# Prompt attention: probabilities transposed by a product with a diagonal of reciprocal row sums

## What is computed

```python
def sparse_attend(q, kg, vg, valid):
    ...
    s = jnp.einsum('btkgd,btjkd->btkgj', qg, kg).astype(jnp.float32) * HEAD_DIM ** -0.5
    s = jnp.where(valid[:, :, None, None, :], s, -1e30)
    pr = jax.nn.softmax(s, axis=-1)
    o = jnp.einsum('btkgj,btjkd->btkgd', pr.astype(vg.dtype), vg)
```

## Time and profile before

| what | value |
| --- | --- |
| time of the kernel, median of 3 runs | 3674.19 us |
| lowest and highest of them | 3671.43 and 3676.53 us |
| span of the profiled execution | 3673.0 us |
| mean granted TensorE clock in it | 0.889 |
| TensorE's matmuls busy | 3060.5 us (83%) |
| VectorE busy | 1360.5 us (37%) |
| ScalarE busy | 741.1 us (20%) |
| GpSimd busy | 933.8 us (25%) |

### The profile page before, as it was taken

How to read it: one execution, slowest core, us unless ns; L and a number is a source line. 1 busy time by engine, 2 the same in 40 slices (tenths; PEclk the granted TensorE clock), 3 DMA queues, 4 the chain that set the end, 5 groups by cost and what they waited for, 6 DMA issues and landing times.

```text
span 3673.0 us, 44605 instructions
## 1 busy us (share of the span) xinstructions
PE 3060.5 (83%) x17464; PEld 2770.9 (75%) x17464; DVE 1360.5 (37%) x1847; ACT 741.1 (20%) x1136; POOL 933.8 (25%) x588
## 2 busy tenths in 40 slices
PE   6999276667799999999999860278888999999996
PEld 5998156666689999999999320134578899999996
DVE  6631644443542222222511177775203422222225
ACT  3321411112110000000200256424311200000001
POOL 2432022220233333333433010000002233333331
PEclk8999678887799999999999575589868999999998
DMA  4111000001211111111211110000122111111111
GB/s 132 46 46 29 17 1 0 0 0 49 76 35 46 46 43 46 46 46 46 90 46 33 50 38 20 0 22 2 55 72 76 32 46 43 46 46 43 46 46 61
DMA packets 237187, 152.44 MB, mean 42 GB/s; under 512 B 21243, under 2 KB 232884, under 8 KB 236169
## 3 DMA queue, kind: packets, MB, share of 16 engines
q1 hardware_dynamic: 226000, 121.17, 11.5%
q10 hardware_dynamic: 11116, 30.33, 2.3%
HBM read 133.46 MB, written 18.01 MB: 41 GB/s over the span
## 4 chain that ended last, share of the span: by engine, by line
PE 69%; DVE 11%; ACT 5%; issue 2%; DMA 0%; DVEq 0%; ACTq 0%; POOL 0%; POOLq 0%
PE ps L1298 50%; ACT junk L815 2%; PE ps L1389 2%; PE ps L1396 2%; PE ps L644 2%; PE ps L713 2%; PE ps L677 1%; PE ps L1347 1%; DVE sc L944 1%; PE ps L1401 1%; DVE hl L2028 1%; ACT dn_yy L1658 1%; PE ps L615 1%; PE ps L746 1%; PE ps L601 1%
## 5 line engine op out<-in xcount | busy, mean ns | idle before, releaser
L1189 POOL TENSOR_TENSOR w_hi<-w_raw,ones 128x512 fp32r<-128x512 f32 (+1 forms) x250 | 370.9, 1484 | 2216.3 <-PE ps L1298 1973.2
L1298 PE MATMUL ps<-xh,w_hi 128*128 128x352 f32 x2928 | 638.4, 326 | 59.3 <-DVE xl L1979 20.7
L1298 PE MATMUL ps<-xh,w_lo 128*128 128x352 f32 x2928 | 634.5, 324 | 0.0
L1298 PE MATMUL ps<-xl,w_hi 128*128 128x352 f32 x2928 | 633.8, 325 | 0.0
L1298 PEld LDWEIGHTS ps<-xh,w_hi 128*128 128x128 f32 x2928 | 502.6, 190 | 63.7 <-issue 59.9
L1298 PEld LDWEIGHTS ps<-xh,w_lo 128*128 128x128 f32 x2928 | 505.8, 189 | 0.0
L1298 PEld LDWEIGHTS ps<-xl,w_hi 128*128 128x128 f32 x2928 | 500.5, 189 | 0.0
L1192 POOL TENSOR_TENSOR w_lo<-w_raw,w_hi 128x512 fp32r<-128x512 f32 (+1 forms) x250 | 480.5, 1922 | 19.6
L2044 DVE TENSOR_TENSOR x<-x,ps 128x1056 f32<-128x1056 f32 x128 | 160.5, 1254 | 501.8 <-PE ps L1298 501.8
L1298 PE MATMUL ps<-hh,w_hi 128*128 128x352 f32 x1536 | 333.0, 325 | 13.7 <-DVE hl L2028 13.7
L1298 PE MATMUL ps<-hh,w_lo 128*128 128x352 f32 x1536 | 331.1, 323 | 0.0
(11 more groups left out here) (363 smaller groups left out, 3100.9 us busy)
## 6 DMA issues: line engine op xcount, KB each, us to landing
w_raw<-in_w_up SPq DMA_DIRECT2D x64, 512.0 KB, 4.1
w_raw<-in_w_down SPq DMA_DIRECT2D x128, 256.0 KB, 2.8
w_raw<-in_w_in_rec SPq DMA_DIRECT2D x24, 512.0 KB, 3.9
x_spill<-x ACTq DMA_DIRECT2D x2, 4224.0 KB, 13.2
x<-x_spill ACTq DMA_DIRECT2D x4, 2112.0 KB, 8.3
w_raw<-in_w_in_att SPq DMA_DIRECT2D x16, 512.0 KB, 3.8
kpg<-in_cache_k SPq DMA_DIRECT2D x64, 128.0 KB, 2.0
vpg<-in_cache_v SPq DMA_DIRECT2D x64, 128.0 KB, 2.0
```

The source lines that it names most:

```text
L1189: pool.tensor_tensor(w_hi[:, j % 2, 0:n], w_raw[:, j % 2, 0:n], ones[:, 0:1].to_broadcast([P, n]), ALU.mult).then_inc(w_hi_done, 1)
L1298: mm = pe.matmul(ps[:, 3 * (j % 2) + t, 0:n], w[:, j % 2, k * P:(k + 1) * P], r[:, k, c0:c0 + n], start=(k == 0 and p == 0), stop=(k == kt ...
```

## The change

The multiplication of pr by the reciprocals is gone. Instead VectorE makes, for each head, a 128x128 diagonal matrix of the reciprocal row sums (scale_q, the identity times the column of reciprocals), with one reciprocal instruction for the four heads. TensorE's transpose of a block of pr becomes an ordinary product of that block with the diagonal matrix, whose result is the transposed block, each query's column scaled by its reciprocal. scale_q has two buffers, for even and odd groups; a new wait keeps VectorE from overwriting one before the value products of the group two before are done. at_nrm now counts diagonals. The samples' attention is unchanged.

```diff
+        scale_q = at("scale_q", [P, 2, GRP, P], F32, M0 + 16 * ROW)
...
                         for g in range(GRP):
-                            mm = pe.transpose(quad(4 + c % 2)[:, g, :], pr[n % 2][:, g, k * P:(k + 1) * P], ident[:, :])
+                            mm = pe.matmul(quad(4 + c % 2)[:, g, :], pr[n % 2][:, g, k * P:(k + 1) * P], scale_q[:, n % 2, g, :],
+                                           start=True, stop=True)
                         mm.then_inc(S["at_tr"], 1)
...
             def normalise(n):
-                w = P * (n // KV + 1)
+                a = n * GRP
+                dve.wait_ge(S["at_exp"], a + GRP)
+                if n >= 2:
+                    dve.wait_ge(S["at_pv"], steps_before[n - 1])
+                own.then(dve.reciprocal(rden[:, a % 8:a % 8 + GRP], den[:, a % 8:a % 8 + GRP]))
                 for g in range(GRP):
-                    a = n * GRP + g
-                    dve.wait_ge(S["at_exp"], a + 1)
-                    own.then(dve.reciprocal(rden[:, a % 8:a % 8 + 1], den[:, a % 8:a % 8 + 1]))
-                    dve.tensor_scalar(pr[n % 2][:, g, 0:w], pr[n % 2][:, g, 0:w], rden[:, a % 8:a % 8 + 1], None, ALU.mult)\
+                    dve.tensor_scalar(scale_q[:, n % 2, g, :], ident[:, :], rden[:, (a + g) % 8:(a + g) % 8 + 1], None, ALU.mult)\
                         .then_inc(S["at_nrm"], 1)
```

## The result

| | median | lowest to highest |
| --- | --- | --- |
| before, 7 runs | 3675.27 us | 3671.43 to 3681.28 |
| after, 7 runs | 3686.35 us | 3683.14 to 3692.16 |
| ratio | 1.0027 | interval 1.0017 to 1.0038 |

The change costs 11.1 us by the medians; 9.3 were predicted. (The ratio and its interval are an estimate of their own, not the quotient of the medians.) The time lies in the range of 3677 to 3692, and 0.4 us above the 3681 to 3686 that were held to be likeliest. The profiled execution of after has a span of 3687.4 us (its own time is 3689.27) and a mean clock of 0.891. Its span is 14.4 longer than that of before, more than the medians are apart, and not all of it comes from the change: the stage's first score product already stands 6.15 later (2364.68 for 2358.53), where both programs are the same. The stage has therefore to be measured from its own start.

What follows compares the result with a forecast made beforehand. In prompt attention VectorE bounds passes 0 to 6, TensorE later ones. VectorE -7.3, early first sets +3.6 and +0.8, open late sets +17.6, clock -5.4 give +9.3 us on 3674.2: 3684, range 3677 to 3692.

Steps and rivals of the forecast that it cites:

- The bounds: Prompt attention: VectorE's queue sets main-loop passes 0 to 6, while masks are built; from pass 7 the chain follows TensorE.
- VectorE's saving: Passes 0 to 6: normalising a group takes 0.99 us at any width, saving 7.3 us; later savings are worth nothing.
- The price of a set: TensorE, four heads' products replacing four transposes: 0.90 us for 0.44, so 0.45 more at full clock, 0.91 at half.
- a product that costs hardly more: Rival, late loop: a product costs hardly more than a transpose, kernel gets faster, 3662 to 3667; chance 0.08, shared with slack.
- that of four times: Rival: a product costs four times a transpose, 1.76 us for four heads; +67 us, 3741; chance 0.02.
- The count of open sets: Passes 7 to 15: 39 four-head groups of products not covered by VectorE's work, at 0.45 us each, 17.6 us.
- The first two sets: Passes 7 to 14: two four-head groups of products need 1.80 us, narrowly covered by VectorE's last maximum and copy, 1.98.
- The new waits: VectorE's waits for earlier value products and for the last of four exponentials before the single reciprocal: cost nothing.
- The first sets: Passes 0 to 6, first four-head products before VectorE's copy: 3.6 us in passes 0, 1, 2, 4; 0.8 in 3, 5, 6.
- The clock: Early passes: shorter TensorE waits remove three of five clock falls of some 1.8 us each, -5.4; bounds none and all.
- The clock does as before: Rival: all five clock falls behind TensorE's early waits stay; +14.7 us, 3689; chance 0.20.
- The clock stays up: Rival: no clock falls from pass 3 on, -10 instead of -5.4; +4.7 us, 3679; chance 0.15.

Runs made afterwards that it cites:

- e1: The changed kernel with the old transposes: VectorE builds diagonals nobody uses, the division by row sums is left out; 3667.12 us, 0.9976 of before.
- e2: The kernel before, VectorE still normalising, with each transpose made by an fp32 product with the identity; 3698.77 us, 1.0063 of before.
- e3: The change for groups 0 to 7 only, groups 8 to 15 as in the kernel before; 3668.96 us, 0.9978 of before.
- e4: The change for groups 8 to 15 only, groups 0 to 7 as in the kernel before; 3693.31 us, 1.0047 of before.
- e5: The kernel before plus unread filling products on TensorE ahead of its waits in groups 3 to 8; 3669.07 us, 0.9981 of before.
- e7: The kernel before with the multiplication by reciprocals of groups 0 to 7 moved to ScalarE, transposes kept; 3655.59 us, 0.9939 of before.

## Why the prediction was right

**The bounds** were read rightly. e1 and e2 show it from both sides: VectorE's saving is worth nothing late (e1: +0.37, all of it the copy's wait in pass 8), and TensorE's price is paid in full there (e2: +17.72). e3 and e4 then put the gain and the loss where the prediction had them.

**VectorE's saving.** A normalisation takes 0.99 to 1.00 at either width, as worked out, and e1's passes 0, 2 and 6 are shorter by that.

**The price of a set** was 0.89 against 0.44, as the neighbouring rows had it. The rival of a product that costs hardly more is out, and so is that of four times: the section Terms of the Trainium skill's "TensorE: Matmul & The Clock Gate" has transpose mode four times faster for FP32, and the measured factor for blocks of 128x128x128 is 2.0.

**The count of open sets**, 39, gave 17.6; measured are 18.09. The excess is the 0.38 behind pass 7, which e1 has without any product and of which 0.30 is the unexplained wait of the copy, and 0.01 to 0.06 a pass elsewhere. The first two sets stay covered: in passes 9 to 14 TensorE is idle for 0.16 to 0.43 us before the value product. In pass 7 no idle time is left, but the value product still starts 0.84 us behind the copy (2465.68 to 2466.52), where it was 0.83.

**The new waits** cost nothing, as argued. The one gap in front of a diagonal's reciprocal is that of group 0, 0.52 us, and since its work is shorter it ends only 0.04 later in the stage than the old normalisation did.

**The first sets** early: +4.4 predicted, +3.80 in e2. The price of 0.91 is borne out in passes 0 and 2 alone; that the sum of the others comes near is luck, since the clock moved them. (Twice 0.90 less 0.87 is 0.93 and not 0.91, a matter of 0.1 us.)

**The clock** is the step of the prediction that does not hold, and that it came out near in size is luck. The prediction let the lengths of the waits decide and took three of five falls to be gone: those behind the waits of 3.90, 5.46 and 4.24. The new lengths were foreseen to 0.5 us or better, and yet the clock fell behind 2.90 and 2.97 and not behind 3.64. Two of the five falls were gone in this execution. Pass 1, where the prediction had nothing, gave 1.90 more, because before's profiled execution was at half clock there and after's was not; e4 and e5, with before's code, were not either. So 5.4 was taken, and some 6 stand in the table of passes, from other passes in part.

What the runs showed in its place is that waits of this length leave the clock to the execution: e3 and after, with the same code and the same wait to 0.01 us, differ. What decides in each stays open. In the medians the clock's gain is what is left beside the work, and not well known: 2.2 us in e1 (-9.2, where +0.4 late and -7.3 are work), 4.1 in after (+11.1, where -2.9 and +18.1 are work) and 5.3 in e3 (-7.3, where -2.9 and the +0.9 of pass 7 are work). The filling gives less: it is worth 8.0 to before and 7.4 to after, so that the change would have taken only 0.6 of the clock's cost away. Each of these medians has an interval of some 3.5 us to either side. Against the forecast of 9.3, the 11.1 has 0.5 more from the late passes; the other 1.3 is, by subtraction, a smaller gain of the clock.

**The rivals.** "The clock does as before" (+14.7) lies above the interval's upper end of 0.38% (14.0), but barely; the profiled execution of after has two falls fewer than that of before. How often that is so, no run shows, and with a gain as small as the filling's 0.6 this rival would be close. "The clock stays up" (+4.7) lies below its lower end (0.17%, 6.2). The reason named for it is not borne out here: Part 4 of the Trainium skill's "TensorE: Matmul & The Clock Gate" says that transpose mode doesn't engage the full clock as products do, but in e2, where all transposes are products, the clock fell behind every one of the five waits, and late, with transposes in a third of the loop, it stays at 1.00 (before).

## What to carry to other kernels

A mean busy share hid two stages with opposite bounds; the same edit was worth -7 us in one (e3) and +17 in the other (e4), and splitting it by loop index (e3) kept the gain alone. Work that two engines share out is best priced where each is on the path, and the engine to give it to is the one that is idle in that very stage: here neither of the two in the change, but ScalarE (e7, 0.9939). And a gain that comes through the clock is to be counted with a wide bound, since the same instructions had it in one execution and not in another.

## What was not expected of the hardware

- The granted clock behind equal waits: 1.00 behind 3.64 us in after, 0.50 behind 3.63 in e3, with the same instructions around them; and pass 1 of the same code at 0.50 (before) and 0.99 (e4). In e5 it fell behind 2.11. What decides it was not settled: the executions differ in when the stage begins, and nothing here varied that alone.
- Filling TensorE's waits with products whose result nobody reads made the kernel before 8.0 us faster by the medians (ratio 0.9981 [0.9972, 0.999]).
- A reciprocal of four columns occupies VectorE's queue for 0.08 us when the next instruction needs nothing of it (e7), and 0.20 when the next waits for its result (after, 2438.35 to 2438.55).
